# Decoder layer on one core: three of four w_b_out blocks in seven products

## The reference

```python
z = xn @ w_in                                   # u, v, b_gate, c_gate, x_in, r_a, r_b
y_a = (gelu(u) * spatial_mix(layer_norm(gelu(v)))) @ w_a_out
y_b = (b_gate * short_conv(c_gate * x_in, conv_w)) @ w_b_out
h = sigmoid(r_a) * y_a + sigmoid(r_b) * y_b
x = x + rms_norm(h @ w_o, mix_post_g)
f = (silu(xn2 @ w_gate) * (xn2 @ w_up)) @ w_down      # xn2 = rms_norm(x, ffn_pre_g)
x = x + rms_norm(f, ffn_post_g)
```

## Time and profile before

| | us |
|---|---|
| median of 3 runs | 1611.36 (1611.17 to 1612.21) |
| profiled execution, its time | 1611.54 |
| its span | 1609.8 |
| PE busy | 1599.3 |
| DVE busy | 1015.6 |
| POOL busy | 677.8 |
| ACT busy | 547.3 |

### The profile page before, as it was taken

One profiled execution on the slowest core, in us unless ns is written; L12 is line 12 of the kernel. 1 busy time (PEld: TensorE's weight loads), 2 busy tenths in 40 slices (PEclk: granted clock), 3 DMA queues, 4 the chain that ended last, 5 costly groups with the idle time before them and its releaser, 6 DMA issues.

```text
span 1609.8 us, 30196 instructions
## 1 busy us (share of the span) xinstructions
PE 1599.3 (99%) x12499; PEld 1551.2 (96%) x12499; DVE 1015.6 (63%) x1410; ACT 547.3 (34%) x836; POOL 677.8 (42%) x487
## 2 busy tenths in 40 slices
PE   9999999999999999999999999999999999999998
PEld 6889999999999999999978899999999999999997
DVE  8757857587583338864435676766666666675766
ACT  4223332222223335322234632222222233452544
POOL 1011434444444444633320325544444443555475
PEclk9999999999999999999999999999999999999999
DMA  6202011321313334452323403533333345572723
GB/s 217 77 1 80 27 53 34 99 79 34 99 60 107 106 106 132 152 187 78 106 105 124 139 27 101 157 104 104 104 106 106 105 125 171 168 237 80 237 105 133
DMA packets 146771, 175.92 MB, mean 109 GB/s; under 512 B 7035, under 2 KB 129523, under 8 KB 146635
## 3 DMA queue, kind: packets, MB, share of 16 engines
q1 hardware_dynamic: 146475, 173.96, 33.6%
q10 hardware_dynamic: 160, 0.04, 0.0%
HBM read 129.52 MB, written 44.49 MB: 108 GB/s over the span
## 4 chain that ended last, share of the span: by engine, by line
PE 98%; DVE 1%; ACT 0%; issue 0%; POOL 0%; DVEq 0%; POOLq 0%; ACTq 0%
PE ps L402 94%; PE ps L511 1%; PE ps L437 1%; PE ps L495 0%; PE ps L651 0%; PE ps L635 0%; PE ps L412 0%; DVE tp L1701 0%; DVE v_smp L1738 0%; PE ps L489 0%; DVE tp_f L2420 0%; DVE small L1671 0%; DVE small L1672 0%; ACT tp_f L1636 0%; DVE x_norm L1689 0%
## 5 line engine op out<-in xcount | busy, mean ns | idle before, releaser
L402 PE MATMUL ps<-tp,ring_hi 128*128 128x258 f32 x7340 | 1190.5, 283 | 0.2 <-issue 0.2
L402 PEld LDWEIGHTS ps<-tp,ring_hi 128*128 128x128 f32 x7340 | 1017.2, 190 | 0.4 <-issue 0.4
L402 PE MATMUL ps<-tp,ring_lo 128*128 128x258 f32 x3670 | 749.6, 283 | 0.0
L402 PEld LDWEIGHTS ps<-tp,ring_lo 128*128 128x128 f32 x3670 | 575.0, 190 | 0.0
L1062 POOL TENSOR_TENSOR ring_lo<-stage,ring_hi 128x512 fp32r<-128x512 f32 (+1 forms) x202 | 308.3, 1535 | 443.2 <-ACT ring_hi L1205 442.8
L1062 POOL TENSOR_TENSOR ring_lo<-ring_f,ring_hi 128x512 fp32r<-128x512 f32 (+1 forms) x216 | 304.5, 1430 | 345.7 <-DVE ring_f L1789 196.7
L1205 ACT ACTIVATE ring_hi<-ring_f 128x512 fp32r<-128x512 f32 (+1 forms) x216 | 135.0, 627 | 481.3 <-DVE ring_f L1784 186.5
L1205 ACT ACTIVATE ring_hi<-stage 128x512 fp32r<-128x512 f32 (+1 forms) x202 | 123.3, 618 | 141.4 <-PE ps L402 86.3
L1781 DVE TENSOR_TENSOR ring_f<-stage 128x512 f32<-128x512 f32 (+1 forms) x54 | 43.0, 796 | 155.8 <-PE ps L402 81.4
L402 PE MATMUL ps<-tp 128*128 128x512 f32 (+1 forms) x384 | 72.1, 340 | 0.0
L1802 DVE TENSOR_TENSOR s_a<-ps,s_a 128x516 f32<-128x516 f32 (+1 forms) x55 | 37.7, 686 | 52.2 <-PE ps L402 51.6
(11 more groups left out here) (237 smaller groups left out, 1394.2 us busy)
## 6 DMA issues: line engine op xcount, KB each, us to landing
stage<-in_w_in SPq DMA_DIRECT2D x24, 1024.0 KB, 5.8
ht_dram<-ht SPq DMA_DIRECT2D x44, 258.0 KB, 4.4
hid_dram<-hq SPq DMA_DIRECT2D x40, 258.0 KB, 3.0
stage<-in_w_gate SPq DMA_DIRECT2D x10, 1024.0 KB, 6.3
stage<-in_w_up SPq DMA_DIRECT2D x10, 1024.0 KB, 5.4
tp_f<-hid_dram SPq DMA_DIRECT2D x16, 516.0 KB, 5.7
tp_f<-ht_dram SPq DMA_DIRECT2D x16, 516.0 KB, 8.6
stage<-in_w_down SPq DMA_DIRECT2D x8, 1024.0 KB, 8.0
```

What stands on the lines that cost most here:

```text
L402: ins = pe.matmul(o, w, xc, start=first and n == 0, stop=last and n == 2)
```

## The change

- Of w_b_out only block 28 stays plain; blocks 29, 30 and 31 take the form of seven products, with gates after `c11`, `c22`, `c12`, `c21` (`b_gate`) as w_a_out has them.
- They need four differences of the B operand's quarters. DVE forms them in each B run (`b_total`, into the new tile `bt`), three ahead of `c21` and one behind its product. SP stores them to `bt_dram` behind the load of block b + 2, loads them back during block 27 (`bt_load`), ACT and DVE split them (`bt_split`, `bt_rest`) in block 28.
- All eight slots of `tp` are now needed during these blocks. The slots are numbered anew (`SLOT_A`, `SLOT_M`). The result h is laid out by `mp` (`h_of`, `H_SLOT`), and its quarters for `mp` 1, 2, 3 are written when the last block's product 1, 2, 3 has freed a slot; w_o's blocks are loaded as slots and ring places come free in block 31.
- POOL gathers the sample columns for w_o in 16 small copies instead of 8.

```diff
-SLOT_A = [7, 5, 6, 0, 4, 1, 2, 3]
+SLOT_A = [6, 0, 1, 7, 2, 3, 4, 5]
+SLOT_M = [2, 0, 1, 6, 3, 4, 7, 5]
+H_SLOT = [0, 2, 3, 1]
...
-QORDER.update({b: (1, 3, 0, 2) for b in range(B_B, B_F + 2)})
+QORDER.update({b: (1, 3, 0, 2) for b in (B_B, B_F, B_UP0)})
...
+                if kind == 2:
+                    for i, t in enumerate(HT_ORDER):
+                        sp.wait_ge(ht_ready, 4 * mp + i + 1)
+                        sp.dma_start(bt_dram[t, :, :, mp, :], bt[:, t]).then_inc(ht_saved[t], 16)
...
+            def bt_load(t):
+                sp.wait_ge(ht_saved[t], 16 * MP)
+                sp.wait_ge(prod_done, done(B_B - 1, 3 + t))
+                sp.dma_start(slot_f(SLOT_M[4 + t], 1), bt_dram[t]).then_inc(total_in[t], 16)
...
-                elif m != 2:
-                    sp.wait_ge(prod_done, done(B_F - 1, {1: 1, 3: 1, 4: 2, 5: 3, 6: 3, 7: 3}[m]))
+                else:
+                    sp.wait_ge(prod_done, done(B_F - 1, {2: 1, 1: 3, 3: 4, 4: 4, 5: 5, 6: 6, 7: 6}[m]))
...
+                act.wait_ge(prod_done, done(B_F - 1, mp - 1) if mp else done(B_B, 1))
+                act.activation(h_of(n, 0, mp), g[:, 2 * mp + n // 2, n % 2], ACT.Copy).then_inc(h_hi, 1)
...
+            bt_split(0)
+            prepare(B_B + 1, 0, 2)
+            bt_split(1)
+            prepare(B_B + 1, 2, 4)
+            bt_split(2)
+            prepare(B_B + 1, 4, 6)
+            bt_split(3)
+            prepare(B_B + 1, 6)
+            s1(B_B + 1)
+            for i in range(4):
+                h_split(0, i)
+            prepare(B_B + 2)
+            s1(B_B + 2)
+            prepare(B_B + 3)
+            s1(B_B + 3)
+            for mp in (1, 2):
+                for i in range(4):
+                    h_split(mp, i)
+            o_split(0)
+            o_split(2)
+            for i in range(4):
+                h_split(3, i)
+                if i:
+                    o_split((1, 3, 4)[i - 1])
+            for m in (5, 6, 7):
+                o_split(m)
...
-                dve.wait_ge(b_ready, 4 * mp + 2)
+                dve.wait_ge(b_ready, 4 * mp + 3)
+                b_total(mp, 0, q[:, 1], q[:, 0])
+                b_total(mp, 2, q[:, 3], q[:, 1])
+                dve.wait_ge(ht_ready, 4 * mp + 1)
+                b_total(mp, 1, q[:, 3], bt[:, 0])
                 c21(r, s_b[:, :])
                 dve.wait_ge(c21_done, SIDX[r])
                 dve.tensor_tensor(q[:, 2], s_b[:, :], q[:, 2], MUL).then_inc(b_ready, 1)
+                dve.wait_ge(b_ready, 4 * mp + 4)
+                dve.wait_ge(ht_ready, 4 * mp + 3)
+                b_total(mp, 3, q[:, 2], bt[:, 1])
+
+            def b_total(mp, t, x, y):
+                if mp:
+                    dve.wait_ge(ht_saved[t], 16 * mp)
+                dve.tensor_tensor(bt[:, t], x, y, SUB).then_inc(ht_ready, 1)
...
+            def b_gate(r, i, src, ready):
+                mp, n = r - B_B, (0, 3, 1, 2)[i]
+                part = g[:, 2 * mp + n // 2, n % 2]
+                dve.wait_ge(ready, SIDX[r])
+                dve.wait_ge(gate_in[n], 16 * (MP + mp + 1))
+                dve.tensor_tensor(src, src, q[:, n], MUL).then_inc(a_gated, 1)
+                dve.wait_ge(a_gated, 4 * (MP + mp - 2) + i + 1)
+                dve.tensor_tensor(part, part, src, ADD).then_inc(h_ready, 1)
+
+            for mp, r in enumerate(range(B_B + 1, B_F), 1):
+                last = r == B_F - 1
+                sums(r + 1, 0)
+                dve.wait_ge(h_ready, 4 * mp)
+                if last:
+                    for step in range(4, 9):
+                        h_rest(step)
+                c11(r, s_b[:, :])
+                b_gate(r, 0, s_b[:, :], c11_done)
+                u1(r)
+                u3(r, s_c[:, :])
+                sums(r + 1, 1)
+                if mp == 1:
+                    h_rest(0)
+                    h_rest(1)
+                elif last:
+                    h_rest(9)
+                    h_rest(10)
+                u2(r)
+                dve.wait_ge(h_ready, 4 * mp + 1)
+                c22(r, s_b[:, :])
+                sums(r + 1, 2)
+                b_gate(r, 1, s_b[:, :], c22_done)
+                if mp == 1:
+                    h_rest(2)
+                    h_rest(3)
+                elif last:
+                    h_rest(11)
+                    h_rest(12)
+                c12(r, s_c[:, :])
+                sums(r + 1, 3)
+                b_gate(r, 2, s_c[:, :], c12_done)
+                if last:
+                    h_rest(13)
+                dve.wait_ge(h_ready, 4 * mp + 2)
+                c21(r, s_b[:, :])
+                b_gate(r, 3, s_b[:, :], c21_done)
+            h_rest(14)
+            h_rest(15)
```

More of the change, by code:

```diff
@@ L410, in turn_norm @@
                 for k in range(KT):
-                    at_k = k ^ 1 if i else k
+                    at_k = k ^ 1 if i and not home(V_TILES[i])[0] else k
                     ins = pe.transpose(ps[:, xn_bank(i) + k // 4, 128 * (at_k % 4):128 * (at_k % 4) + rows],
@@ L618, in _ @@
                     product(r, p)
[L619 to L622, removed]
+            for i in range(4):
+                bank_free(B_B - 1, PLAIN_BANK[i])
+                half(B_B, i, PLAIN_BANK[i], lambda q: (b_lo, (3, 1, 4, 2)[q]))
+            for r in range(B_B + 1, B_F):
+                for p in range(7):
+                    if r == B_B + 1 and p in (1, 3, 4, 6):
+                        pe.wait_ge(b_lo, (1, 3, 4, 6).index(p) + 5)
+                    product(r, p)
             def o_part(i, j, k):
@@ L638, in o_part @@
                     b, gg, off = home(t)
-                    x_h, x_l = (tp[:, 2 * a + b, part, gg, kp, off:off + 128] for part in range(2))
+                    x_h, x_l = (tp[:, H_SLOT[kp], part, gg, 2 * a + b, off:off + 128] for part in range(2))
                     outs = [ps[:, O_BANK[i] + n, :] for n in range(2)]
@@ L1078, in _ @@
                 pool.wait_ge(ready, 16)
[L1079 to L1082, removed]
+                for k in range(KT):
+                    src = tp[:, H_SLOT[k // 2], part, :, 2 * (k % 2):2 * (k % 2) + 2, 256:CS]
+                    dst = smp_o[:, k, 32 * part:32 * part + NS].rearrange("p (g b i) -> p g b i", g=2, b=2)
+                    pool.tensor_copy(dst, src).then_inc(o_packed, 1)
             prepare(B_F)
@@ L1150, in xn_prompt @@
             b, gg, off = home(t)
-            return tp[:, 0:6:5, part, gg, :, off:off + 128] if b else tp[:, 6:8, part, gg, :, off:off + 128]
+            return tp[:, 0:8:7, part, gg, :, off:off + 128] if b else tp[:, 1:7:5, part, gg, :, off:off + 128]
         def turned(bank):
@@ L1160, in x1n_both @@
             return g[:, a::2, b].rearrange("p k g c -> p g k c")
-        H_STEPS = [(mp, n) for mp in range(MP) for n in QORDER[B_B]]
+        H_STEPS = [(mp, n) for mp in range(MP) for n in h_order(mp)]
         @block.scalar
@@ L2153, in _ @@
-            h_rest(4 * MP - 1)
+                dve.tensor_tensor(h_of(n, 1, mp), g[:, 2 * mp + n // 2, n % 2], h_of(n, 0, mp).bitcast(f32), SUB).then_inc(h_lo, 1)
+            for i, n in enumerate(QORDER[B_B]):
+                part, tmp = g[:, n // 2, n % 2], (s_b, s_c)[i % 2]
+                dve.wait_ge(prod_done, done(B_B, i))
+                dve.wait_ge(gate_in[n], 16 * (MP + 1))
+                if i >= 2:
+                    dve.wait_ge(h_ready, i - 1)
+                dve.tensor_tensor(tmp, reg(PLAIN_BANK[i], both), q[:, n], MUL).then_inc(pl_dve, 1)
+                dve.wait_ge(pl_dve, PL_DVE[B_B] + i + 1)
+                dve.tensor_tensor(part, part, tmp, ADD).then_inc(h_ready, 1)
+                sums(B_B + 1, i)
+                bt_rest(i)
```

106 lines of the change are left out of this document (44 added, 62 removed).

## The result

The changed kernel takes 1634.42 us (median of 4 runs, 1633.27 to 1634.98) where the kernel before took 1611.48 on the same chip: 1.0141 times as long, 95% interval 1.0123 to 1.0158. The forecast was 1618.3 with a range of 1612 to 1626: slower was right, the size was not.

A forecast was written before the change was run, and what follows sets the result against it. TensorE, busy 1599.3 of 1609.8 us, was taken as the bound, so time follows the number of matmuls. 1611.54 - 8.7 + 12.6 + 2.8 = 1618.3 us, range 1612 to 1626.

The forecast's parts named there:

- Term 1: Last w_b_out blocks: three blocks each lose one product of 2.89 us, -8.7 us.
- Term 2: Four B runs: differences ahead of c21 delay store, load and c11, so PE waits about 3 us each, +12.6 us.
- The turns: B runs: DVE's differences alternate with POOL's subtractions, starting 1.70 us apart, making the load 5.1 us late.
- rival C: B runs: bt_dram stores behind the 1 MB load delay its landing about 3 us, four times: 1630 us, chance 0.08.
- behind it in the same queue: Ground against the stores slowing the load: they stand behind it in one queue.
- PE waits 2.9 us: First run behind a B run: c11 done at 302.05, while PE could start its sixth product at 299.16.
- rival D: PE's clock falls in each 3 us wait, losing 2.6 us four times, +10.4: 1628.7 us, chance 0.07.
- Rivals B and E: Differences slip between POOL's subtractions: all, 1605.6 us, chance 0.08; or one or two at once, 1611, chance 0.12.
- just covered: Bank X in the B runs: c21 frees it at 293.2, PE wants it at 293.4.
- Term 3: Into w_o: PE waits for late blocks, 0.9 us at the fourth, +2.8 us in all, bounds 0 to 5.2.
- the walk: Step-by-step timing of the start of w_o, with loads landing some 3.5 us after issue; PE waits 2.8 us.

The follow-up runs named there:

- 4: Kernel before plus only the four differences on VectorE in each B run and their bt_dram stores, never read back: 1636.06 us, 1.0154 of before.
- 1: Changed kernel, with the load of block b + 2 in the B runs issued ahead of the fourth ob_dram store: 1609.58 us, 0.9986 of before.
- 6: Changed kernel with all four differences behind the fourth product, SyncE's queue as in the change: 1608.68 us, 0.9986 of before.
- 3: Changed kernel with the bt_dram stores of the first three B runs issued behind the next block's load as well: 1631.63 us, 1.0126 of before.
- 2: Changed kernel with 24 idle matmuls added after product 5 of the four runs behind the B runs: 1627.32 us, 1.0103 of before.
- 7 to 9: Single w_o steps: c12 right behind c22, on 1; ScalarE's high parts copied earlier, on 1; GpSimd's low parts held, on 6: 1610.15, 1609.61, 1608.34 us.
- 10: Kernel of 9 with h low-part steps 4 to 11 all ahead of c11 and w_o block 4 copied one place earlier: 1605.91 us, 0.9966 of before.
- 9: Kernel of 6 with GpSimd's low parts of w_o held until block 31's first gate addition: 1608.34 us, 0.9980 of before.
- 5: Changed kernel with two differences ahead of c21 in each B run and two behind the fourth product: 1624.87 us, 1.0086 of before.

## Why the prediction was right and wrong

- **Term 1** (-8.7) was right to 0.1: three blocks in 60.77 us where three times 20.25 was forecast.
- **Term 2** had the mechanism right and the size wrong: +26.2 for +12.6. The turns came as walked: `c21` began its 0.68 at 292.57 (forecast: done at 293.2), the load was issued 5.2 us late (5.1). Shown by 4 (this part alone makes the loss), 1 and 6 (either way of issuing the load in time removes it). Two things were missing. The load landed 1.0 later, 0.9 of it for the `bt_dram` stores behind it (rival C in kind, not in size: it had about 3 us a run; shown by 3; I had set "behind it in the same queue" against it), so the waits are 15.5 instead of 12.6. And the failed step: "PE waits 2.9 us" was priced as if the work behind it ran at full pace. What the runs showed in its place: the granted clock fell to 0.50 in all four waits and cost 10.3 us by the clock rows (10.7 with all that isn't waiting). That is rival D, chance 0.07, priced at 10.4; 2 shows it, by removing the fall without removing the lateness. Without it the time would have been 1634.4 - 10.7 = 1623.7, within the range of 1612 to 1626; without the later load alone, 1631.5, not. That D's price hits is in part luck: it took 5.2 us at half pace for each wait from a start of the kernel where the earlier trace rows show a granted clock of 1.00 in both windows and only the counts of matmuls differ, and the four stretches were 3.3 to 6.0 us, 5.2 in the mean. My ground for the low chance of D was that the longest wait of before, 0.84 us, did no harm; waits 4 to 5 times as long are no neighbours of that row, and the Trainium skill's warning (TensorE: Matmul & The Clock Gate, section Why this matters for your kernels) speaks of gaps of about this size. The traces now agree with it: the clock fell in 4 of 4 waits of 3.46 to 4.37 us.
- **Rivals B and E** needed differences that slip in between GpSimd's subtractions: of the three that run beside them none did, in any of the traces (1.67 to 1.80 us each; the fourth, with GpSimd idle, took 0.70). That bank X was "just covered" was right too: 0.2 us to spare.
- **Term 3**: +4.5 for +2.8, within its bounds (0 to 5.2). The late fourth and fifth block came (0.54 and 1.58 for 0.9 and 1.9), with w_o's loads landing 3.2 to 4.7 us after their issue where the walk took 3.5. By the start times of PE's rows, the three places cost 1.7, 0.8 and 1.8 us. Not foreseen was bank Y: GpSimd's first two subtractions held up both operations of the first gate (the walk had it hold up one), so `c12` came late (1.56). 7 to 9 show that none of the three single steps tried shortens the stage by more than 0.4 us; the order of 10, which changes several at once, does.
- **Block 58** (+1.3) was in no term. ScalarE waited 2.95 us there for the second `hid_dram` load, 1.86 before. In the profiles of the ten variants with products in w_b_out it is 0.7 to 2.3; in the one without (4) 0.1. I didn't find the cause; it stays open.

## What to carry to other kernels

Look at what a late instruction holds up in a DMA queue before its own length: a store and a load in program order carried 5 us of lateness on VectorE, which had time to spare, into four runs of TensorE, at 6.5 us each. Price a wait of TensorE of over 2 us with the slow pace behind it, which here cost as much as two thirds of the wait, and look for it by narrow windows, since the page's clock row hid it. Where VectorE and GpSimd take turns, moving one operation can move the turn to the next (9); here only a new order of the whole stretch paid (10).

## What the runs showed of the hardware

- TensorE's granted clock fell to 0.50 with all waits of 2.28 us and more (up to 4.4), and with one of 2.17; with another of 2.17 it stayed full, as with single waits of 2.0 at w_o (1, 3, 5). It also fell with a wait of 2.02 that had one of 1.08 ahead of it, 4.5 us of work between (2); whether the 1.08 was needed for that isn't shown. In the changed kernel the slow pace lasted 3.3 to 6.0 us.
- With 24 matmuls in the wait, and 0.6 to 1.3 us of it left idle, the clock stayed full behind all four (2).
- A 1 MB load landed 6.93 us after issue with four 258 KB stores issued right behind it, 6.07 with another 1 MB load and only then the stores (3).
- A VectorE operation on two SBUF tensors that met GpSimd's ended only after GpSimd's: 1.7 us beside 512 columns, up to 2.8 beside 1024, 0.55 us behind its end in the rows shown; one with a PSUM input beside it kept its 0.68 (`c21` at 292.57).
